# Layer 1 adds its gated expert rows into the output by the scatter; the overflow tile runs behind its own expert

## What is computed

```
grp_p, grp_idx = top_k(softmax(h @ w_grp + b_grp), 1)            # one of 4 groups
top_p, top_j   = top_k(softmax(exp_logits of that group), 2)     # two of its 8 experts
gates   = grp_p * top_p / sum(top_p)                             # two gates a token
experts = grp_idx * 8 + top_j
for every (token, expert):  y = (silu(h @ w1[e]) * (h @ w3[e])) @ w2[e]     # 1024 -> 512 -> 1024
out[token] = sum over its two experts of gate * y
```

## Time and profile before

| | us |
|---|---|
| median of three runs (lowest to highest) | 1585.29 (1584.35 to 1585.72) |
| the profiled execution: its time | 1585.1 |
| its span, first to last instruction | 1583.3 |
| TensorE busy in it | 1334.0 (84%) |
| VectorE, ACT, POOL busy | 443.3, 323.7, 268.2 |

### The profile page before, as it was taken

The page is one execution under the profiler, slowest core; times in us unless marked ns, Lnnn a source line. Parts: engine busy times, 40 slices in busy tenths (PEclk is TensorE's granted clock), DMA queues, the critical chain, the costliest instruction groups (busy, mean ns, idle before and its releaser), DMA issues.

```text
span 1583.3 us, 20571 instructions
## 1 busy us (share of the span) xinstructions
PE 1334.0 (84%) x8048; PEld 770.9 (49%) x8048; DVE 443.3 (28%) x957; ACT 323.7 (20%) x638; POOL 268.2 (17%) x370
## 2 busy tenths in 40 slices
PE   7998898998777777774899999999999777777873
PEld 3443456665444444442556666556565444344441
DVE  2898444111010101012344544436111010101002
ACT  3564231000000000001344444322000000000000
POOL 3887000211111111100000000000111111111100
PEclk9999899999999999997899999999999999999997
DMA  8513128999999999996700401436999999999995
GB/s 293 171 44 160 53 93 339 423 420 423 424 425 424 425 424 424 424 422 265 262 1 1 160 1 46 167 127 254 422 421 424 424 424 425 424 425 424 422 414 215
DMA packets 73202, 473.40 MB, mean 299 GB/s; under 512 B 16198, under 2 KB 20294, under 8 KB 38840
## 3 DMA queue, kind: packets, MB, share of 16 engines
q1 hardware_dynamic: 60760, 443.67, 68.2%
q0 software_dynamic: 10080, 16.35, 2.8%
q10 hardware_dynamic: 2304, 12.58, 2.0%
HBM read 465.93 MB, written 23.33 MB: 309 GB/s over the span
## 4 chain that ended last, share of the span: by engine, by line
PE 46%; DMA 41%; DVE 6%; POOL 3%; ACT 2%; issue 1%; SPq 0%; ACTq 0%; POOLq 0%; DVEq 0%
DMA ring<-in_moe_w 36%; PE banks L1454 11%; PE banks L1470 7%; PE banks L1574 6%; PE banks L1603 4%; PE banks L1371 4%; POOL scratch L552 2%; DMA area<-in_moe_w 2%; DVE banks L940 2%; PE banks L1278 2%; PE banks L1357 2%; PE banks L1663 2%; PE banks L1618 1%; PE banks L1298 1%; DMA scratch<-xn_dram,at_in 1%
## 5 line engine op out<-in xcount | busy, mean ns | idle before, releaser
L1454 PE MATMUL banks<-ring,scratch 128*64 128x256 f32 x3776 | 431.5, 382 | 99.4 <-DMA ring<-in_moe_w 96.2
L1454 PEld LDWEIGHTS banks<-ring,scratch 128*64 128x64 f32 x3776 | 285.8, 137 | 263.6 <-DMA ring<-in_moe_w 102.0
L1470 PE MATMUL banks<-ring,scratch 128*64 128x512 f32 x960 | 222.6, 605 | 67.1 <-DMA ring<-in_moe_w 65.0
L1111 DVE COPY scratch<-banks 128x256 f32<-128x256 f32 x65 | 27.6, 424 | 800.8 <-PE banks L1462 800.8
L1470 PEld LDWEIGHTS banks<-ring,scratch 128*64 128x64 f32 x960 | 75.1, 138 | 176.9 <-issue 168.8
L747 ACT ACTIVATE scratch<-banks 128x256 f32<-128x256 f32 x65 | 24.9, 383 | 518.3 <-PE banks L1454 515.1
L1574 PE MATMUL banks<-hT,ring 128*128 128x512 f32 x256 | 120.2, 614 | 0.8 <-DVE hT L894 0.8
L1278 PE MATMUL banks<-hT,ring 128*128 128x512 f32 x256 | 113.1, 602 | 0.8 <-DVE hT L894 0.8
L582 POOL COPY at_out<-rows_out 128x1 int32 (+1 forms) x58 | 10.5, 181 | 594.3 <-ACT scratch L751 594.3
L751 ACT ACTIVATE scratch<-banks 128x512 f32<-128x512 f32 x65 | 38.8, 597 | 344.0 <-PE banks L1470 344.0
L552 POOL TENSOR_TENSOR scratch<-scratch 128x512 f32<-128x512 f32 x77 | 97.9, 1272 | 18.7 <-ACT scratch L714 8.8
(11 more groups left out here) (227 smaller groups left out, 1213.8 us busy)
## 6 DMA issues: line engine op xcount, KB each, us to landing
ring<-in_moe_w SPq DMA_DIRECT2D x178, 2048.0 KB, 27.2
area<-in_moe_w SPq DMA_DIRECT2D x12, 2048.0 KB, 14.7
ring<-in_attn_w_qkv SPq DMA_DIRECT2D x6, 2048.0 KB, 20.3
hT<-in_moe_w SPq DMA_DIRECT2D x5, 2048.0 KB, 17.1
area<-y_dram ACTq DMA_DIRECT2D x8, 1024.0 KB, 7.9
ring<-in_conv_w_in SPq DMA_DIRECT2D x4, 1024.0 KB, 11.2
ring<-in_conv_w_in SPq DMA_DIRECT2D x2, 2048.0 KB, 15.8
ring<-in_conv_w_out SPq DMA_DIRECT2D x2, 2048.0 KB, 23.3
```

Of the source, the lines that this page charges most:

```text
L1454: last = mm(bank[2 + s][q * SLOTS:(q + 1) * SLOTS, k * 256:(k + 1) * 256], xeT[s][:, c % 4, c // 4, :], wc[:, c, q * 256:(q + 1) * 256], s ...
L1470: last = mm(bank[6 + s][q * SLOTS:(q + 1) * SLOTS, :], hidT[s][:, j % 2, j // 2, :], w2c[:, j, q * 512:(q + 1) * 512], start=j == 0, stop= ...
```

## The change

- Both layers: the main loop has 33 turns (TURNS). The last expert that overflows, if its number is at least EARLY (9), changes places with the one at place HELD (26), and turn 27 is its overflow tile, computed from the same w1, w3 and w2 in the ring. If there is none, turn 27 runs with empty lists. SP reads each place's expert from `ctl`, which now holds the order too. Overflow tiles beyond that run behind the loop as before.
- Both layers: the one-hot arithmetic is in bfloat16, with token numbers cut into two exact parts, so `lists` has 16 matmuls instead of 8, and `lists2` 16 or 24, in the middle of step 1. Some VectorE steps for the exchange stand before `take_first`, and the gates are computed before the second list.
- Layer 1 (SUMMED): `y_dram` is the output itself. POOL stores `x_res` to it before the experts run, four stores of 512 KB. The second list carries the gate of each row in place of its output row; ACT scales the rows by it as it evicts them; the scatter goes to the token's own row and adds (`compute_op=ALU.add`). Each scatter waits until the one before it has landed, since two may hit the same row. Reload, sums and final stores of layer 1 go.

```diff
-TILES = EXPERTS + OVER
+TURNS = EXPERTS + 1
+TILES = TURNS + OVER
+HELD = 26
+EARLY = 9
+ORDER = 1 + OVER
+SUMMED = (1,)
...
-        y_dram = [nc.dram_tensor(f"y_dram{l}", [2 * ASSIGN, D // 2], F32, kind="Internal").ap() for l in range(LAYERS)]
+        y_dram = [nc.dram_tensor(f"y_dram{l}", [2 * T if l in SUMMED else 2 * ASSIGN, D // 2], F32, kind="Internal").ap() if l == 0 or l not in SUMMED
+                  else out[0].rearrange("t (h f) -> (t h) f", h=2) for l in range(LAYERS)]
...
@@ SP: the weights
+                sp.wait_ge(ctl_done, l + 1)
+                def at_place(p):
+                    return sp.value_load(ctl[0:1, bass.ds(p + ORDER, 1)], min_val=0, max_val=EXPERTS - 1)
+                def used(p):
+                    return p + (1 if p < HELD else 2)
...
-                def loop_units(s, e):
-                    down_to_ring(3 * s, e, y, e - 1)
-                    to_ring(3 * s + 1, w1_of(e + 2), w1_used, e + 1)
-                    to_ring(3 * s + 2, w3_of(e + 2), up, e + 1)
+                def loop_units(s, p, y_used, up_used):
+                    down_to_ring(3 * s, at_place(p), y, y_used)
+                    e = at_place(p + 2)
+                    to_ring(3 * s + 1, w1_of(e), w1_used, up_used)
+                    to_ring(3 * s + 2, w3_of(e), up, up_used)
...
+                for p in range(HELD - 1, EXPERTS - 4):
+                    loop_units((p - 1) % 2, p, used(p - 2), used(p))
...
@@ SP: the end
+            if 1 in SUMMED:
+                for s in range(2):
+                    sp.wait_ge(y_stored[1][s], 16 * (EXPERTS // 2 + 1 - s))
+                sp.wait_ge(moe_over, 2)
...
@@ POOL
+                    if l in SUMMED:
+                        g.indirect_dma_start(out=y_dram[l][:, :],
+                                             out_offset=bass.IndirectOffsetOnAxis(ap=at_out[:, s:s + 1], axis=0),
+                                             in_=y_sb[s], in_offset=None,
+                                             bounds_check=y_rows[l] - 1, oob_is_err=False, compute_op=ALU.add).then_inc(done, 16)
...
                 def last_scatter(s, e, wait_at):
...
                     pool.wait_ge(m["y_taken"], e + 1)
+                    if l in SUMMED:
+                        pool.wait_ge(y_stored[l][1 - s], 16 * ((e + 1) // 2))
...
+                def scatter(s, e, wait_at, other_stored):
                     pool.wait_ge(m["y_taken"], e + 1)
...
+                    if l in SUMMED and other_stored is not None:
+                        pool.wait_ge(y_stored[l][1 - s], other_stored)
...
+                if l in SUMMED:
+                    for t in range(NT):
+                        pool.wait_ge(x_done, X_DONE[l] + t + 1)
+                        g.dma_start(y_dram[l][2 * t * P:2 * (t + 1) * P, :].rearrange("(p h) f -> p (h f)", h=2),
+                                    x_res[:, t, :]).then_inc(x_stored, 16)
...
@@ ACT
+                if l in SUMMED:
+                    a.activation(y_sb[s], bank[6 + s][:], ACT.Copy, scale=gate_rows[:, bass.ds(tile, 1)]).then_inc(sems["y_taken"], 1)
...
@@ VectorE, routing, before take_first(l, 0)
+                link(v.tensor_scalar(late_cmp, tiles_base, 0.0, None, ALU.is_gt))
+                link(v.tensor_reduce(late, late_cmp, AX.X, ALU.add))
+                link(v.tensor_scalar(late_is, late, float(EARLY), None, ALU.is_ge))
+                link(v.scalar_tensor_tensor(late_d, late, -float(HELD), late_is, ALU.add, ALU.mult))
+                link(v.tensor_scalar(late_e, late_d, float(HELD), None, ALU.add))
+                link(v.tensor_scalar(v8(0), v8(0), 99.0, None, ALU.add))
+                link(v.tensor_scalar(v8(6), v8(0), late_e, late_d, ALU.is_equal, ALU.mult))
+                link(v.tensor_scalar(v8(7), v8(0), float(HELD), late_d, ALU.is_equal, ALU.mult))
+                link(v.tensor_tensor(v8(7), v8(7), v8(6), ALU.subtract))
+                link(v.tensor_tensor(v8(0), v8(0), v8(7), ALU.add))
+                link(v.scalar_tensor_tensor(v8(5), v8(3), float(EXPERTS), v8(2), ALU.add, ALU.add))
+                link(v.scalar_tensor_tensor(v8(5), v8(5), late_is, v8(0), ALU.subtract, ALU.subtract))
                 take_first(l, 0)
-                link(v.tensor_scalar(v8(0), v8(0), 99.0, None, ALU.add))
-                link(v.scalar_tensor_tensor(v8(5), v8(3), float(EXPERTS - 1), v8(2), ALU.add, ALU.add))
-                link(v.tensor_tensor(v8(5), v8(5), v8(0), ALU.subtract))
...
@@ VectorE, after take_first(l, 1): gates, then the second list's factors, then ctl
+                if l in SUMMED:
+                    all_gates = gates[:].rearrange("p k t -> p (k t)")
+                    link(v.tensor_copy(gate_part[0], all_gates))
+                    link(v.tensor_tensor(gate_rest, all_gates, gate_part[0], ALU.subtract))
...
+                for b in range(n_second - 1):
+                    link(v.tensor_tensor(hot_part[b], hot_tile, bt(second[b], TILES), ALU.mult))
+                v.tensor_tensor(hot_tile, hot_tile, bt(second[n_second - 1], TILES), ALU.mult).then_inc(hot_done, 1)
...
@@ VectorE, end of the layer
+                if l in SUMMED:
...
+                    return
...
@@ TensorE
                 up_step(0, 0, in_ring(0), in_ring(1))
                 lists(l)
-                lists2(l)
-                step(1, 1, in_ring(2), in_ring(3), in_ring(4), first=True)
+                step(1, 1, in_ring(2), in_ring(3), in_ring(4), first=True, between=lambda: lists2(l))
...
+                step(HELD, 0, *up_units(HELD), down_unit(HELD - 1))
+                step(HELD + 1, 1, *up_units(HELD), down_unit(HELD))
+                for p in range(HELD + 1, EXPERTS - 2):
+                    step(p + 1, (p + 1) % 2, *up_units(p), down_unit(p - 1))
```

More of the change, by code:

```diff
@@ L176, in trunk @@
         over_xe = [sem(f"over_xe{l}") for l in range(LAYERS)]
-        over_y = [sem(f"over_y{l}") for l in range(LAYERS)]
+        x_stored = sem("x_stored")
         over_w = [[sem(f"over_w{l}_{k}") for k in range(3)] for l in range(LAYERS)]
@@ L491, in _ @@
                         lambda: None)
[L492 to L495, removed]
+            if 1 in SUMMED:
+                for s in range(2):
+                    sp.wait_ge(y_stored[1][s], 16 * (EXPERTS // 2 + 1 - s))
+                sp.wait_ge(moe_over, 2)
+            else:
+                for t in range(NT):
+                    sp.wait_ge(x_done, X_DONE[1] + NT + t + 1)
+                    sp.dma_start(out[0, t * P:(t + 1) * P, :], x_res[:, t, :]).then_inc(out_stored, 16)
+                sp.wait_ge(out_stored, 16 * NT)
         @block.gpsimd
@@ L572, in last_scatter @@
                     alone(pool)
[L573 to L578, removed]
+                    put_rows(s, y_stored[l][s])
+                def scatter(s, e, wait_at, other_stored):
@@ L1096, in route @@
                 link(v.tensor_tensor(gates[:, 1, :], gates[:, 0, :], v4(4), ALU.mult))
+                if l in SUMMED:
+                    all_gates = gates[:].rearrange("p k t -> p (k t)")
+                    link(v.tensor_copy(gate_part[0], all_gates))
+                    link(v.tensor_tensor(gate_rest, all_gates, gate_part[0], ALU.subtract))
+                    link(v.tensor_copy(gate_part[1], gate_rest))
+                    link(v.tensor_tensor(gate_rest, gate_rest, gate_part[1], ALU.subtract))
+                    link(v.tensor_copy(gate_part[2], gate_rest))
+                    second = gate_part
+                else:
+                    second = [assign2[:, b].rearrange("p k t -> p (k t)") for b in range(2)]
@@ L1098, in take_xT @@
+                dve.wait_ge(lists2_ready, l + 1)
+                if l in SUMMED:
+                    v.tensor_copy(gate_rows[:], bank[6][:, 0:TILES]).then_inc(lists2_done, 1)
+                else:
+                    v.tensor_scalar(rows_out[:], bank[6][:, 0:TILES], far_out[:], None, ALU.add).then_inc(lists2_done, 1)
             def take_xT(l, sems, s, e1):
@@ L1490, in up_step @@
                     up(s, 0, w1[0]).then_inc(m["w1_used"], 1)
+                    between()
                     pe.wait_ge(w3[1], w3[2])
@@ L1503, in down_step, with step @@
                     down(m, s, w2[0], e + 1).then_inc(m["y_ready"], 1)
-                def step(e, s, w1, w3, w2, first=False):
-                    up_step(e, s, w1, w3)
+                def step(e, s, w1, w3, w2, first=False, between=lambda: None):
+                    up_step(e, s, w1, w3, between)
                     if first:
```

234 lines of the change are left out of this document (142 added, 92 removed).

## The result

The changed kernel takes 1574.71 us (median of four runs, 1573.02 to 1575.79), the kernel before 1584.82 (four runs): the ratio on record is 0.9943, 95% interval 0.9931 to 0.9955 (the quotient of the two medians is 0.9936). The forecast was 1569.4. The profiled execution after has a span of 1573.8 us against 1583.3: 9.5 us less, where the sum said 15.9. It is followed here from the start to the end.

What follows compares the result with a forecast made beforehand. Full DMA (424 GB/s) bounds the expert loops, TensorE early in each. Terms -17.3 - 17.5 + 11.5 + 7.4 = -15.9 take 1585.1 to 1569.2, as median 1569.4 us; range 1555 to 1589 (0.8), likeliest case 1562 to 1577.

Steps and rivals of the forecast that it cites:

- Overflow tile: Layer 0's end: overflow tile and its 6 MB reload behind the loop go, what follows moves up; -17.3 us (16.0 to 17.4).
- done would come 3 us after the last scatter's issue: Sign at layer 0's end: the done mark comes about 3 us after the last scatter's issue.
- Extra turn: Both expert loops, now 33 turns: the added 11.61 us TensorE step hides behind queued weight units; 0, up to 11.6 a layer otherwise.
- never empty: Around the held turn: the DMA queue's stock of weight units outlasts each late slot, so the stream never stops.
- the prediction's own list: Wrong if layer 0 doesn't gain some 13 us net, layer 1's steps don't lengthen by 0.4, or DMA idles at the held turn.
- Stream of layer 1: Layer 1's expert loop: adding reads each destination row, costed as another gather on full DMA; +11.5 us (10 to 13).
- Routing: Before each layer's first expert: twelve VectorE operations delay it 2.0 us, TensorE's lower clock adds 1.7; +7.4 us for both layers.
- Tail of layer 1: Layer 1's end: reload, sums and final stores go, three scatters land one after another; -17.5 us (-19.4 to -15.1).
- the end is the last scatter's landing: Layer 1's tail: nothing follows the last scatter's landing at 1565.8; the end comes within 4 us of its issue.
- free reads: Rival, layer 1's stream: adding costs it nothing, the 11.5 falls away; 1558 us, 1554.5 if the clock holds; chance 0.20.
- dear adding: Rival, layer 1's scatters: adding costs 0.94 us of DMA time a turn or more, kernel slower, up to 1625; chance 0.16.
- the turn that shows: Rival, each layer's end: the extra turn's 11.6 us is not hidden; 1593 us, 1581 if in one layer; chance 0.08.

Runs made afterwards that it cites:

- The third experiment: Changed kernel with EARLY 99 instead of 9, so expert 19's second tile runs behind layer 0's loop again and turn 27 is empty: 1590.31 us (1.0039).
- the early take: Changed kernel with one line moved: VectorE evicts the first expert's rows ahead of the twelve new routing operations; 1567.08 us (0.9899).
- no sum: Changed kernel with SUMMED empty: layer 1 scatters ungated rows to rows of their own, reloads and sums them as before; 1576.12 us (0.9947).
- the last kernel above: Changed kernel with first expert's rows evicted before the new operations, the lists' eight iotas behind the start's mark, and SUMMED empty: 1568.23 us (0.9896).
- the first experiment: Changed kernel with layer 1's scatters writing instead of adding, every wait and the gate kept: 1561.19 us (0.9863).
- the two experiments: Kernel before with late POOL work after layer 1's sums: a store to a scratch tensor, 1588.20 us (1.0022), or one memset, 1587.31 us (1.0016).

## Why the prediction was right, and where its size was off

The direction and the signs of the four terms hold, and the overflow tile and the routing went as described. The sum was 6.4 us too favourable in the profiled execution, most of it in one step, the end of layer 1's tail.

- *Overflow tile:* -17.3 forecast. From the last regular down, read in both traces, the last scatter has landed 7.5 us later (722.62 + 2.3), where done came 24.9 later before: -17.4. Attention's first matmul comes 31.6 after it instead of 49.2: -17.6. The third experiment gives 17.6 at the same matmul and 15.6 in whole time. Right, but for the sign that done would come 3 us after the last scatter's issue: it came after 1.0, because without an overflow tile POOL marks done without waiting for the landing.
- *Extra turn:* 0 forecast. From layer 0's first expert to its last regular down are 457.3 us before, 458.7 after, and 458.0 with the early take; in layer 1 460.1, 461.3 (no sum) and 458.7 (early take, the adding's 12.4 taken off). What shows is the first expert's lower clock; the turn itself is within 1 us of nothing. The cleanest pair is the kernel before and the last kernel above (both repairs, no sum), which keeps the turn and has neither the lower clock nor the adding: 457.3 against 457.6 in layer 0, 460.1 against 460.1 in layer 1. So the 0 is right, but the working behind it is not: the queue was to be "never empty", and the engines idled around the held turn (0.94 and 0.77 busy, the lines above; 0.97 in 640 to 660 and 0.89 in 1454.6 to 1474.6 in that last kernel). By the prediction's own list that was a sign of being wrong. Why the stock ran out is open.
- *Stream of layer 1:* +11.5 forecast from the gather's row; 12.4 measured. Per step 0.49 instead of 0.40. The size was right, the picture behind it is not shown, so the nearness is in part luck: I took the cost as a fetch of the old rows, and the page counts no byte of one. What shows is twice the data packets, each of half the bytes and of no less time; a fetch that the profile doesn't count is not excluded. The Trainium skill, in "Collectives: The Full Stack" under "The bandwidth ceiling", says of ReduceScatter that its add needs two source reads on one ring and so halves the rate; it does not speak of scatters. The trace agrees with the rate: the data packets of plain scatters took 10.3 us of all 16 engines, those of adding ones 23.3, a rate of 0.44. It shows no second source in the counted bytes.
- *Routing:* +7.4 forecast. The twelve operations took 2.67 us (1082.56 to 1085.23), the first expert starts 2.4 later in each layer behind what came before it, and the streams behind end 1.4 and 1.3 later still: 7.5 in all. In layer 1 the low clock cost more on the first expert itself, 2.9 instead of 1.7, and the stream absorbed some of it.
- *Tail of layer 1:* -17.5 forecast, -12.8 measured (27.0 from the last down to the end before, 14.1 after). This is the step that failed: "the end is the last scatter's landing". The landing itself was foreseen: 5.8 us after the last down ends, and it was 6.1. But the program ends 4.4 us behind it, because POOL closes; the end was to follow the last scatter's issue in 4 us and took 8.1. Of the tail's 4.7 us that is 4.4 and the chained landings 0.3.
- *Left out:* the five iotas more in POOL's constants. They gate the first transpose: +1.06. I went through the diff from the routing on and took the set-up as free.

Together: -17.6 - 12.8 + 12.4 + 7.5 + 1.1 = -9.4, against -9.5 in the spans. With the two terms missed (4.7 and 1.1) the forecast's sum is -10.1. Of the rivals, free reads and dear adding are settled by the first experiment, the turn that shows by the streams of the kernel without sum and lower clock.

The change as it stands is thus nearly all overflow tile. The sum in the scatters is a trade of 12 us of a full stream against 13 of a tail.

## What to carry to other kernels

Price a transfer that adds by its time on the DMA engines, not by bytes: beside a full stream each adding scatter cost 0.4 to 0.5 us more than a plain one, and so it pays only where it shortens a tail by more than the stream it lengthens; here one layer broke even and the other lost 11 us. When a change makes another engine the last to work, look at how long that engine takes to close, and in the profile before at what it hid behind. New work goes behind what an idle engine waits for: one moved line was worth 7.6 us.

## What was not expected of the hardware

- POOL's closing drain lasts 5.9 to 7.7 us, after a memset as after a scatter; late work there moved the end by 3.6 us (a store) and 2.7 (a memset) in the two experiments; in the changed kernel the end came 4.4 after the last landing.
- Adding scatters leave the counted bytes and memory reads unchanged (455.71 MB with and without), but their data goes in 2048-byte packets of 182 ns instead of 4096-byte ones of 161, which takes 13.4 us more of all DMA engines for 33 scatters; and each occupies POOL 1.60 us instead of 1.03.
- After 3.2 us of standing, TensorE worked at the 1.2 GHz level (0.50) for at least 6 us in layer 1; after 0.85 us its first expert took the 7.13 us of before. At the start of attention the same kernel fell to the lower level in one execution (13.03 us) and not in another (10.57).
